# Gate columns of the spread stage formed token by token on VectorE, with the row mask laid out for an in-order cast

## What is computed

```python
top_s, top_i = lax.top_k(s, P_TOPK)                      # 16 of 128 keys, per head, per half
cand_i = top_i[:, :, 0, :, None] * P_KEYS + top_i[:, :, 1, None, :]
best_s, best_pos = lax.top_k(cand_s, P_TOPK)
expert = jnp.take_along_axis(cand_i, best_pos, axis=-1)  # 8 heads x 16 picks a token
gate = jax.nn.softmax(best_s, axis=-1)
a = jnp.einsum('td,thkd->thk', hb, expert_u[expert])
act = jax.nn.gelu(a, approximate=False) * gate
return jnp.einsum('thk,thkd->td', act, expert_v[expert])
```

## Time and profile before

| | us |
|---|---|
| median of 3 runs | 3537.25 |
| lowest and highest | 3533.98, 3540.88 |
| the profiled execution, device time | 3545.49 |
| its span from first to last instruction | 3543.7 |

### The profile page before, as it was taken

How to read it: one execution, slowest core, us unless ns; L and a number is a source line. 1 busy time by engine, 2 the same in 40 slices (tenths; PEclk the granted TensorE clock), 3 DMA queues, 4 the chain that set the end, 5 groups by cost and what they waited for, 6 DMA issues and landing times.

```text
span 3543.7 us, 51514 instructions
## 1 busy us (share of the span) xinstructions
PE 3300.5 (93%) x18470; PEld 2844.1 (80%) x18470; DVE 2497.5 (70%) x5310; ACT 1079.8 (30%) x1689; POOL 1762.4 (50%) x1341
## 2 busy tenths in 40 slices
PE   8999996999997999367799999999999999999999
PEld 6888885556655999366689999998998899899898
DVE  3111103444331899899489999999999999999998
ACT  3222212343430222399522222222222222222221
POOL 0000004322220346200378888888878788888785
PEclk9999997999998999799999999999999999999999
DMA  4222215222214000065989999999999999999997
GB/s 176 101 92 101 94 63 209 76 103 87 96 63 149 21 19 18 17 174 160 309 330 368 379 370 368 380 369 350 382 362 361 362 373 368 376 375 368 360 372 285
DMA packets 338482, 831.47 MB, mean 235 GB/s; under 512 B 25904, under 2 KB 132784, under 8 KB 336048
## 3 DMA queue, kind: packets, MB, share of 16 engines
q0 software_dynamic: 129024, 469.82, 35.0%
q1 hardware_dynamic: 180752, 319.86, 25.7%
q10 hardware_dynamic: 28576, 40.31, 3.1%
HBM read 741.09 MB, written 88.80 MB: 234 GB/s over the span
## 4 chain that ended last, share of the span: by engine, by line
PE 46%; DVE 3%; DMA 1%; issue 1%; POOL 0%; SPq 0%; ACT 0%; DVEq 0%
PE exp_up L2077 23%; PE exp_vp L2094 23%; DVE exp_now L2024 1%; DMA scratch_gates<-spr_g 1%; DVE pass_g L2017 0%; DVE pass_g L1995 0%; DVE exp_ring L2017 0%; DMA pass_g<-in_u 0%; DVE exp_up L1981 0%; SPq L1785 0%; DVE exp_am_lo L1986 0%; DVE exp_now L2020 0%; POOL exp_v_lo L1814 0%; POOL exp_u_lo L1809 0%; POOL exp_ring L1823 0%
## 5 line engine op out<-in xcount | busy, mean ns | idle before, releaser
L2077 PE MATMUL exp_up<-dense_h_hi,exp_u_hi 128*128 128x320 f32 x2048 | 640.5, 313 | 23.5 <-POOL exp_u_lo L1809 14.0
L2077 PE MATMUL exp_up<-dense_h_lo,exp_u_hi 128*128 128x320 f32 x2048 | 634.5, 310 | 0.0
L2077 PE MATMUL exp_up<-dense_h_hi,exp_u_lo 128*128 128x320 f32 x2048 | 632.9, 309 | 0.0
L1995 DVE TENSOR_TENSOR pass_g<-pass_g,exp_vp 128x512 f32<-128x512 f32 x640 | 436.2, 682 | 110.1 <-PE exp_vp L2094 107.6
L2094 PE MATMUL exp_vp<-exp_v_hi,exp_am_hi 128*128 128x512 f32 x1280 | 504.5, 394 | 0.0
L2094 PE MATMUL exp_vp<-exp_v_hi,exp_am_lo 128*128 128x512 f32 x1280 | 503.4, 393 | 0.0
L2094 PE MATMUL exp_vp<-exp_v_lo,exp_am_hi 128*128 128x512 f32 x1280 | 501.9, 392 | 0.0
L1809 POOL TENSOR_TENSOR exp_u_lo<-pass_g,exp_u_hi 128x1024 fp32r<-128x1024 f32 x128 | 308.6, 2412 | 262.7 <-ACT exp_u_hi L1869 260.4
L2077 PEld LDWEIGHTS exp_up<-dense_h_hi,exp_u_hi 128*128 128x128 f32 x2048 | 386.4, 189 | 52.4 <-DVE exp_am_lo L1986 12.1
L2077 PEld LDWEIGHTS exp_up<-dense_h_lo,exp_u_hi 128*128 128x128 f32 x2048 | 385.7, 188 | 24.4
L2077 PEld LDWEIGHTS exp_up<-dense_h_hi,exp_u_lo 128*128 128x128 f32 x2048 | 386.3, 189 | 0.0
(11 more groups left out here) (216 smaller groups left out, 6073.1 us busy)
## 6 DMA issues: line engine op xcount, KB each, us to landing
pass_g<-in_u SPq DMA_DIRECT2D x126, 512.0 KB, 8.4
pass_g<-in_v SPq DMA_DIRECT2D x126, 512.0 KB, 6.5
pass_g<-scratch_gates SPq DMA_DIRECT2D x124, 320.0 KB, 6.6
scratch_z<-prj_zo ACTq DMA_DIRECT2D x33, 768.0 KB, 3.5
prj_w_raw<-in_w_in SPq DMA_DIRECT2D x44, 512.0 KB, 4.3
scratch_gates<-spr_g SPq DMA_DIRECT2D x2, 8192.0 KB, 30.4
scratch_gates<-pass_g SPq DMA_DIRECT2D x2, 8192.0 KB, 30.5
mix_zg<-scratch_z SPq DMA_DIRECT2D x9, 1024.0 KB, 5.3
```

The source lines that it names most:

```text
L1995: V.tensor_tensor(acc[:, t, c], acc[:, t, c], vp[:, n % 4, :], ALU.add).then_inc(added, 1)
L2077: last = nc.tensor.matmul(up[:, g, 0:GW], u[a][:, o, k * P:(k + 1) * P], h2[b][:, k, cols(g)], start=(k == 0 and n == 0), stop=(k == KD - ...
```

## The change

`hot_j` and `places_j` go. The gated columns are formed token by token: for each of the 8 tokens one `tensor_scalar` over the 128 f32 place numbers of `iota`, with two operations, "equal to this pick's j" and "times this pick's gate". Both scalars are columns of `rt`, one value for each partition, f32. Only the plane of i is still cast to bf16 (`place[:, 0]`). `iotas` and `hot_i` get the token outside and the place inside, so the comparison repeats each token's i over 128 places and ACT casts without a change of order. `hot_i` is now the only large DVE instruction of a step, and it comes before the columns. A tile `spare` fills the room. DVE's loop over the tiles is written out in full; the other engines keep theirs.

```diff
-        iotas = s.sb("iotas", [P, P, B], BF16)
-        hot_i = s.sb("hot_i", [P, 2, P, B], BF16)
-        places_j = s.sb("places_j", [P, B, P], BF16)
-        hot_j = s.sb("hot_j", [P, 2, B, P], BF16)
+        iotas = s.sb("iotas", [P, B, P], BF16)
+        hot_i = s.sb("hot_i", [P, 2, B, P], BF16)
+        s.sb("spare", [P, 3 * B * P], BF16)
...
-            nc.vector.tensor_copy(place[:, :, :], rt[:, 0:2, :]).then_inc(tables, 1)
-            dve.wait_ge(tables, 3)
+            nc.vector.tensor_copy(place[:, 0, :], rt[:, 0, :]).then_inc(tables, 1)
+            dve.wait_ge(tables, 2)
...
-                    nc.vector.tensor_tensor(hot_j[:, q % 2, :, :], places_j[:, :, :],
-                                            place[:, 1, at(tok, B)].rearrange("p (b o) -> p b o", o=1).broadcast_to([P, B, P]),
-                                            ALU.is_equal).then_inc(hot_j_ready, 1)
                     dve.wait_ge(rows_ready, step + 1)
                     nc.vector.tensor_tensor(hot_i[:, q % 2, :, :], iotas[:, :, :],
-                                            place[:, 0, at(tok, B)].rearrange("p (o b) -> p o b", o=1).broadcast_to([P, P, B]),
+                                            place[:, 0, at(tok, B)].rearrange("p (b o) -> p b o", o=1).broadcast_to([P, B, P]),
                                             ALU.is_equal).then_inc(hot_i_ready, 1)
-                    dve.wait_ge(hot_j_ready, step + 1)
                     dve.wait_ge(spread_ready, step + 1)
-                    nc.vector.tensor_tensor(cols[:, q % 2, :, :], hot_j[:, q % 2, :, :],
-                                            rt[:, 2, at(tok, B)].rearrange("p (b o) -> p b o", o=1).broadcast_to([P, B, P]),
-                                            ALU.mult).then_inc(cols_ready, 1)
-
-            tiles(dve, body)
+                    for b in range(B):
+                        last = nc.vector.tensor_scalar(cols[:, q % 2, b, :], iota[:, :], rt[:, 1, at(tok + b, 1)],
+                                                       rt[:, 2, at(tok + b, 1)], ALU.is_equal, ALU.mult)
+                    last.then_inc(cols_ready, 1)
+
+            for t in range(NTD):
+                body(t, t % 2, t // 2, P)
...
-                    nc.scalar.copy(rows[:, q % 2, :, :], hot_i[:, q % 2, :, :].rearrange("p k b -> p b k")).then_inc(rows_ready, 1)
+                    nc.scalar.copy(rows[:, q % 2, :, :], hot_i[:, q % 2, :, :]).then_inc(rows_ready, 1)
```

More of the change, by code:

```diff
@@ L1553, in spread @@
         rt_in, iota_set, tables = s.sem("rt_in"), s.sem("iota_set"), s.sem("tables")
-        hot_i_ready, hot_j_ready = s.sem("hot_i_ready"), s.sem("hot_j_ready")
+        hot_i_ready = s.sem("hot_i_ready")
         rows_ready, cols_ready = s.sem("rows_ready"), s.sem("cols_ready")
@@ L1606, in _ @@
             dve.wait_ge(iota_set, 1)
-            nc.vector.tensor_copy(iotas[:, :, :], iota[:, :].rearrange("p (k o) -> p k o", o=1).broadcast_to([P, P, B])
-                                  ).then_inc(tables, 1)
-            nc.vector.tensor_copy(places_j[:, :, :], iota[:, :].rearrange("p (o k) -> p o k", o=1).broadcast_to([P, B, P])
+            nc.vector.tensor_copy(iotas[:, :, :], iota[:, :].rearrange("p (o k) -> p o k", o=1).broadcast_to([P, B, P])
                                   ).then_inc(tables, 1)
             dve.wait_ge(rt_in, 16)
-            nc.vector.tensor_copy(place[:, :, :], rt[:, 0:2, :]).then_inc(tables, 1)
-            dve.wait_ge(tables, 3)
+            nc.vector.tensor_copy(place[:, 0, :], rt[:, 0, :]).then_inc(tables, 1)
+            dve.wait_ge(tables, 2)
             def body(t, slot, pair, n):
```

## The result

| | before | after |
|---|---|---|
| median of 5 runs, us | 3537.25 | 3556.1 |
| lowest and highest | 3533.98, 3542.33 | 3549.47, 3556.48 |
| the profiled execution, device time | 3545.49 | 3549.47 |
| its span | 3543.7 | 3547.7 |

A forecast was written before the change was run, and what follows sets the result against it. DVE and ACT were taken as full at the same pace before, DVE alone after. The stage: 1469.9 + 80 x 3.237 + 3.23 = 1732.1, 16.3 us later than 1715.8, giving 3553.5 us, range 3510 to 3575.

The forecast's parts named there:

- DVE alone sets the pace: Spread stage after the change: ACT needs 1.82 us a step and PE 2.05, both under DVE's step.
- Each scalar costs its own fetch: New column instructions: two SBUF scalars cost 0.065 us twice, a DVE step of 3.24 us; chance 0.42.
- t: Start-to-start time of one new tensor_scalar: 0.263 us forecast, break-even 0.217, in a DVE step of 1.13 + 8t.
- the low clock: Tile borders: should PE's clock fall, step 18's columns come some 0.5 us late, five times at most, 0 to 2.5 us.
- The estimate from the Trainium skill, ScalarE: ScalarE's 93 ns per per-partition operand, applied to the column instructions: 0.32 us each, a step of 3.68.
- The one from VectorE: DVE Perf Modes: Column instructions: 58 cycles plus elements, nothing for scalars; the case of t = 0.133, 3481 us, chance 0.05.
- hot_i takes the price of hot_j: Row mask on DVE, each step: 1.13 us in place of 0.60.
- The cast in order: ACT's cast of the row mask: 0.91 us start to start, so ACT needs 1.82 of a step, not 2.86.
- PE keeps 2.05 and its clock: PE's matmuls in each step stay at 2.05 us; low clock throughout was a rival, 3574 us, 0.05 together with fetch.
- The borders: Tile borders: DVE's five waits for PE, 10.5 us, go; PE still idles about 2 us, not 3.2.
- Start and end: Stage's ends: the cast of place saves 0.33 us; from DVE's last columns to the last gate copy's end, 3.23 us.
- The written-out loop at nothing: 720 compute instructions in line instead of a loop body: costed at nothing; a fetch stall would be 0.26 us a step.

The follow-up runs named there:

- `rows_only`: Kernel before with only the mask's place innermost in iotas and hot_i and the cast in order; 3588.03 against 3552.92 us, ratio 1.0088.
- the first comparison: Changed kernel against kernel before, ratio 1.0045; the second, on another chip with more runs, gave 3565.35 against 3551.16 us, ratio 1.0035.
- `pool_cols`: Kernel before with the new mask and in-order cast, hot_j kept on DVE, its product with the gates moved to POOL; 3628.32 against 3552.92 us, ratio 1.0212.

## Why the prediction was right, and where its sizes were off

- *DVE alone sets the pace*: shown. It is busy for all 40 us between borders, ACT waits for hot_i 67 times in 80 steps, and taking scalars away shortened the step by what it took from DVE.
- *Each scalar costs its own fetch*: that each costs its own time is shown, by 0.136, 0.195 and 0.256 us for none, one and two. This was the even bet of the prediction, and what it hung on. One SBUF scalar was priced at 0.065 and costs 0.06; the base was priced at 0.133 and costs 0.136. So t was 0.256, not 0.263, and a step 3.186, not 3.237: 80 x 0.051 = 4.1 us of the sum did not come. With 0.24 less at the start and 0.4 more for the low clock it is the difference between the 16.3 us forecast for the stage and the 12.4 measured. That twice came true at near even odds is in part luck: the reason given, that a fetch is waiting for the memory and a second address a second wait, was not tested. The runs show that the second scalar costs as much as the first, and not what the time is made of.
- The estimate from the Trainium skill, ScalarE: Activation LUTs, section What ACT_TABLE_LOAD costs (each per-partition operand 93 ns), has the right form, two cost twice, and the wrong size for DVE: 0.32 against 0.256. The one from VectorE: DVE Perf Modes, section on the TRN2 errata (58 cycles and the elements, no term for scalars), is 0.127 for two elements a cycle, near the 0.136 of the kernel without scalars, and half of what two scalars make of it.
- *hot_i takes the price of hot_j*: 1.13, right, and `rows_only` shows it by itself. *The cast in order*: 1.00 from start to start, against 0.91 assumed, so ACT needs 1.91 of a step and not 1.82, which changed nothing.
- *PE keeps 2.05 and its clock*: right between the borders.
- *The borders*: DVE's 10.5 us of waits went, right. In the first profile the clock fell behind the borders, and this cost DVE 0.16 us at the first and 0.4 in all, inside the 0 to 2.5 us left for it; in the second it cost nothing. The 0.5 us a border that the prediction allowed doesn't follow from its own figures: rows(16) at 4.2 and 3.4 us of matmuls end at 7.6, where cols(18) starts.
- *Start and end*: the cast of `place` takes 0.49 in place of 0.83, as said. Another 0.24 us went that no step had named: the gap of 0.27 behind that cast is 0.04 now. From the last columns' end to the last gate copy's end it was 3.27, forecast 3.23: PE starts 0.20 us behind the columns, not 0.13.
- *The written-out loop at nothing*: right, measured by itself.
- The median rose by 18.9 us in the first comparison and by 14.2 in the second, where the ratio gives 12.4. The stage says 12.4, so that the forecast of 3553.5 lay so near 3556.1 is partly luck: the stage's 12.4 us put on the median of before would be 3549.7.

## What to carry to other kernels

Before one wide VectorE operation is split token by token, count the SBUF scalars: at 128 f32 elements each of them costs nearly half as much again as the bare instruction, and two of them eat most of what the fused operation saves (eight without scalars take 1.09 us where the two wide operations took 2.27; with two scalars each they take 2.05). Where two engines are full at the same pace, relieving one gains nothing and burdening the other costs at once; look first for a split that shares both costs (here 2 or 4 steps of 16 in the new layout), and for the gaps where both stand still, as at the tile borders, which alone were worth 10.5 us.

## What the runs showed of the hardware beyond that

- VectorE beside GpSimd. In `pool_cols` hot_i, begun 0.16 us ahead of POOL, took 1.14 us, and hot_j, the same operation on the same shapes but begun while POOL ran, took 2.84 from start to start. It ended 1.01 us behind POOL (1541.02 + 2.81 = 1543.83, and hot_i started at 1544.84), as if it had been held until then. The Trainium skill, SBUF — State Buffer, section SBUF: two separate sides, says that a VectorE operation with two SBUF inputs and a GpSimd operation that reads SBUF share a port pair by an exclusive lock, and that the one that starts first keeps it. The hot_j rows agree; whether POOL was held by hot_i at its own start no row tells, as none shows this product without VectorE beside it. Rows of the experts stage of the same kernel show the other side:

```profile
2505.08 2.41 POOL L1810 TENSOR_TENSOR exp_u_lo<-pass_g,exp_u_hi 128x1024 fp32r<-128x1024 f32 x1
...
2505.76 1.23 DVE L2018 CUSTOM_DVE_ANT_0 exp_ring<-exp_now,exp_ring 128x1024 f32<-128x1024 f32 x1
2506.90 0.09 DVE L2018 DVE_READ_ACCUMULATOR2_ANT pass_g<- 128x1 f32 x1
```

  Here a VectorE operation begins while POOL runs and takes 1.14 us all the same. Of its two inputs only `exp_ring` lies in SBUF; `exp_now` is a PSUM tile. So it is not of the kind that the page says is held, and these rows agree too.
- ScalarE's cast of 1024 elements takes 1.95 us where it steps over 8 bf16 elements and 1.00 in order. The Trainium skill, SBUF — State Buffer, section Door 1, says that SBUF is read in lines of 16 bytes and that each access to a new line pays; here each element is a new line, and the rows agree.
